# A two-layer decoder trunk on one core: the sixth weight remainder of an expert on POOL, the overflow placing in thirteen parts, and expert weights read in runs of 4 KB

## The reference, cut to what matters

```
x = x + hierarchical_moe(rms_norm(x, norm_ffn[l]), ...)

# D_MODEL = 1024, D_FF_EXPERT = 256, N_EXPERTS = 16, TOP_K = 2, DEPTH = 2, float32
for e in range(N_EXPERTS):
    hid = jax.nn.silu(t @ w_g[e]) * (t @ w_u[e])
    y = y + gates[:, e:e + 1] * (hid @ w_d[e])
```

## Time and profile before

| | before |
|---|---|
| median of 3 runs | 1600.07 us (1598.69 to 1601.12) |
| the profiled execution, its own time | 1602.11 us |
| its span | 1599.9 us |
| PE busy | 1460.6 us, 91% of the span |
| DVE busy | 931.6 us, 58% |
| ACT busy | 845.0 us, 53% |
| POOL busy | 446.9 us, 28% |
| chain that ended last | PE 67%, DVE 13%, issue 6%, ACT 5%, DMA 5%, POOL 3% |

### The profile page before, as it was taken

How to read it: one execution, slowest core, us unless ns; L and a number is a source line. 1 busy time by engine, 2 the same in 40 slices (tenths; PEclk the granted TensorE clock), 3 DMA queues, 4 the chain that set the end, 5 groups by cost and what they waited for, 6 DMA issues and landing times.

```text
span 1599.9 us, 22011 instructions
## 1 busy us (share of the span) xinstructions
PE 1460.6 (91%) x7636; PEld 1131.9 (71%) x7636; DVE 931.6 (58%) x1844; ACT 845.0 (53%) x1665; POOL 446.9 (28%) x634
## 2 busy tenths in 40 slices
PE   7999999999999995999689999999999999779993
PEld 5786777677767884777477867776677678667772
DVE  3544655534554446999654455645444535579995
ACT  4445555555443335888533555555554433558882
POOL 3314228320000025853005043284000000268210
PEclk9999999999999997999879999999999999989997
DMA  6822222112232366999566212221122332679995
GB/s 154 149 78 55 64 56 66 53 54 63 64 112 76 101 204 223 337 363 354 195 176 120 75 53 63 58 72 53 53 67 60 107 95 98 226 241 346 372 320 195
DMA packets 154325, 226.82 MB, mean 142 GB/s; under 512 B 20547, under 2 KB 89923, under 8 KB 154212
## 3 DMA queue, kind: packets, MB, share of 16 engines
q1 hardware_dynamic: 142724, 205.43, 42.2%
q0 software_dynamic: 10768, 17.80, 3.3%
q10 hardware_dynamic: 720, 2.16, 0.4%
HBM read 216.80 MB, written 25.49 MB: 151 GB/s over the span
## 4 chain that ended last, share of the span: by engine, by line
PE 67%; DVE 13%; issue 6%; ACT 5%; DMA 5%; POOL 3%; SPq 1%; ACTq 0%; POOLq 0%; DVEq 0%
PE bank L488 17%; PE bank L490 16%; PE bank L489 16%; PE bank L1399 4%; DVE xT L553 4%; PE bank L1384 3%; PE bank L1375 3%; PE bank L1377 2%; ACT xT L547 2%; DMA raw<-in_w_in_dram 2%; DVE oT L856 1%; POOL rsq L1970 1%; DMA rows<-ytok 1%; PE bank L1431 1%; PE bank L1434 1%
## 5 line engine op out<-in xcount | busy, mean ns | idle before, releaser
L488 PE MATMUL bank<-wh,xT 128*128 128x512 f32 (+1 forms) x960 | 401.5, 418 | 15.4 <-DVE xT L1743 5.3
L490 PE MATMUL bank<-wh,xT 128*128 128x512 f32 (+1 forms) x960 | 376.6, 392 | 0.0
L489 PE MATMUL bank<-wl,xT 128*128 128x512 f32 (+1 forms) x960 | 375.3, 391 | 0.0
L461 ACT ACTIVATE wh<-raw 128x512 fp32r<-128x512 f32 (+1 forms) x300 | 187.2, 624 | 330.1 <-PE bank L490 314.0
L467 DVE TENSOR_TENSOR wl<-raw,wh 128x512 fp32r<-128x512 f32 (+1 forms) x300 | 214.6, 716 | 245.8 <-ACT wh L461 235.1
L488 PEld LDWEIGHTS bank<-wh,xT 128*128 128x128 f32 x960 | 182.1, 190 | 83.3 <-issue 33.0
L490 PEld LDWEIGHTS bank<-wh,xT 128*128 128x128 f32 x960 | 181.7, 189 | 37.9
L489 PEld LDWEIGHTS bank<-wl,xT 128*128 128x128 f32 x960 | 182.9, 191 | 30.6 <-issue 1.4
L1542 ACT ACTIVATE prob<-prob,nmax 128x128 f32<-128x128 f32 (+3 forms) x192 | 107.2, 560 | 124.5 <-DVE nmax L1755 124.0
L1755 DVE CUSTOM_DVE_ANT_0 prob<-bank,mask 128x128 f32<-128x128 f32 (+3 forms) x128 | 60.6, 489 | 187.6 <-PE bank L1375 98.6
L2078 POOL TENSOR_TENSOR rows<-x_rows,ac 128x512 f32<-128x512 f32 x16 | 21.9, 1405 | 514.6 <-DVE x_rows L1826 514.6
(11 more groups left out here) (328 smaller groups left out, 2545.7 us busy)
## 6 DMA issues: line engine op xcount, KB each, us to landing
raw<-in_w_in_dram SPq DMA_DIRECT2D x192, 256.0 KB, 2.7
bqkv<-in_w_expert_gate_dram SPq DMA_DIRECT2D x64, 256.0 KB, 4.9
bqkv<-in_w_expert_up_dram SPq DMA_DIRECT2D x64, 256.0 KB, 6.0
bqkv<-in_w_expert_down_dram SPq DMA_DIRECT2D x32, 512.0 KB, 7.2
q_c<-in_w_expert_gate_dram SPq DMA_DIRECT2D x64, 256.0 KB, 5.4
q_c<-in_w_expert_up_dram SPq DMA_DIRECT2D x64, 256.0 KB, 6.8
head_odd<-in_w_expert_down_dram SPq DMA_DIRECT2D x32, 512.0 KB, 6.9
raw<-in_w_branch_dram SPq DMA_DIRECT2D x48, 256.0 KB, 2.6
```

Of the source, the lines that this page charges most:

```text
L461: nc.scalar.activation(wh[:, i % HL, 0:width], raw[:, i % RAW, 0:width], ACT.Copy).then_inc(hi_ready, 1)
L488: nc.tensor.matmul(out, lhs[0], rhs[0], start=start, stop=False)
L489: nc.tensor.matmul(out, lhs[0], rhs[1], start=False, stop=False)
L490: return nc.tensor.matmul(out, lhs[1], rhs[0], start=False, stop=stop)
```

## The change

Five things change together.

1. The remainder of pair 5 (the second half of down) of experts 0 to 14 is made by POOL and no longer by DVE, with a semaphore of its own (`last_lo_ready`).
2. POOL's order becomes: four gathers first; then in each step e the remainder of pair 5, the gather of expert e + 4, the scatter of expert e, one part of the placing, and in layer 0 two gains. The placing has thirteen parts (steps 0 to 12) where it had six, with the same operations; its product on PE moves from step 9 to step 13.
3. Gate and up are loaded with four transfers of 512 KB where there were eight of 256 KB, and a partition reads 4 KB in one run where it read runs of 1 KB. A partition then holds rows 8p to 8p + 7 of the weights, and so the token rows are written in that order by POOL (`by_eight`: the same operation with the output strided). Down is loaded in two transfers as before, in runs of 4 KB where there were runs of 2 KB.
4. A pair of down is now one half of the contraction (k) and all 1024 columns, where it was both halves and 512 columns. PE goes through k first: the first half for both halves of the columns, then the second half for both.
5. The semaphore counts follow.

```diff
         def pair_lo(e, j, par, half):
+            eng, done = (nc.gpsimd, last_lo_ready) if j == 5 else (nc.vector, pair_lo_ready)
             pair, landed, count = pair_place(e, j, par, half)
-            nc.vector.wait_ge(pair_hi_ready, of(pair_hi_ready, pair_no(e, j) + 1))
-            nc.vector.wait_ge(landed, of(landed, count))
-            nc.vector.tensor_tensor(pair_w[:, pair_ring(e, j, par), 1], pair,
-                                    pair_w[:, pair_ring(e, j, par), 0].bitcast(F32),
-                                    ALU.subtract).then_inc(pair_lo_ready, 1)
+            eng.wait_ge(pair_hi_ready, of(pair_hi_ready, pair_no(e, j) + 1))
+            eng.wait_ge(landed, of(landed, count))
+            eng.tensor_tensor(pair_w[:, pair_ring(e, j, par), 1], pair,
+                              pair_w[:, pair_ring(e, j, par), 0].bitcast(F32), ALU.subtract).then_inc(done, 1)
...
-        def load_gate_up(sp, expert, j, par, s_):
+        def load_gate_up(sp, expert, quad, par, s_):
+            ms = slice(1024 * quad, 1024 * (quad + 1))
             for half, w in ((0, "w_expert_gate"), (1, "w_expert_up")):
-                src = at(t[w].rearrange("l e (k p) f -> (l e) p k f", p=P), expert)
-                sp.dma_start(pair_raw[par][j][:, :, half * FF:(half + 1) * FF], src[:, 2 * j:2 * j + 2, :]).then_inc(s_, 16)
+                src = at(t[w].rearrange("l e (p k) f -> (l e) p (k f)", p=P), expert)
+                sp.dma_start(gate_up_raw[par][:, half, ms], src[:, ms]).then_inc(s_, 16)
...
         def experts_pe(pe):
...
-                for c in range(2):
-                    j = c if is_const(e, NE - 1) else 4 + c
-                    pos_wait(pe, y_read[c], of(y_read[c], e))
-                    pe.wait_ge(pair_lo_ready, of(pair_lo_ready, pair_no(e, j) + 1))
-                    down(y_bank[c][:], pair_ring(e, j, par)).then_inc(y_done, 1)
+                for k in range(2):
+                    j = k if is_const(e, NE - 1) else 4 + k
+                    pair_split(pe, e, j)
+                    for c in range(2):
+                        if k == 0:
+                            pos_wait(pe, y_read[c], of(y_read[c], e))
+                        mm = down(c, k, pair_ring(e, j, par))
+                        if k or c:
+                            mm.then_inc(y_done, 1)
...
         def experts_act(act):
...
-                act.wait_ge(y_done, of(y_done, 2 * e + 1))
+                act.wait_ge(y_done, of(y_done, 3 * e + 2))
                 pos_wait(act, y_out[par], of(y_out[par], 16 * half))
                 nc.scalar.activation(ysb[:, par, 0:512], y_bank[0][:], ACT.Copy).then_inc(y_read[0], 1)
...
         def experts_dve(dve, layer):
...
                     pair_lo(e, 4, par, half)
-                    pair_lo(e, 5, par, half)
                     silu(e + 1, 1 - par)
...
         def experts_pool(pool, layer):
...
-            for e in range(NE):
-                if e >= 2:
-                    pool.wait_ge(xg_turned, of(xg_turned, 2 * (e - 1)))
-                gather(xg[:, e % 2, :], tab_i[:, e:e + 1], xg_in[e % 2])
-                if e >= 4:
-                    home(e - 4)
-                if 2 <= e < 8:
-                    place_overflow(pool, e - 2)
-                if e >= 4 and layer + 1 < DEPTH:
-                    for q in range(2 * (e - 4), min(N_GAINS, 2 * (e - 3))):
+            for e in range(4):
+                rows_of(e)
+            for e in range(NE):
+                if e < NE - 1:
+                    pair_lo(e, 5, e % 2, e // 2)
+                if e + 4 < NE:
+                    rows_of(e + 4)
+                home(e)
+                place_overflow(pool, e)
+                if layer + 1 < DEPTH:
+                    for q in range(2 * e, min(N_GAINS, 2 * e + 2)):
                         load_gain(pool, layer + 1, q)
```

More of the change, by code:

```diff
@@ L317, in build @@
         RAW_SEMS = [sem(f"raw_in{i}") for i in range(RAW)]
-        pair_in = [[sem(f"pair_in{b}_{j}") for j in range(6)] for b in range(2)]
+        pair_in = [[sem(f"pair_in{b}_{j}") for j in range(4)] for b in range(2)]
         xg_in = [sem(f"xg_in{b}") for b in range(2)]
@@ L373, in build @@
             PER_LAYER[f"y_read{b}"] = NE
-            for j in range(6):
-                PER_LAYER[f"pair_in{b}_{j}"] = (32 if j < 4 else 16) * NE // 2
+            for j in range(4):
+                PER_LAYER[f"pair_in{b}_{j}"] = (32 if j < 2 else 16) * NE // 2
         for n in range(NT):
@@ L616, in body @@
                 expert = sp.value_load(ctl[0:1, bass.ds(c, 1)], min_val=0, max_val=NE - 1)
-                for j in range(4):
-                    load_gate_up(sp, layer * NE + expert, j, 0, ovs[now[0]]["w"])
+                for quad in range(2):
+                    load_gate_up(sp, layer * NE + expert, quad, 0, ovs[now[0]]["w"])
                 for q in range(2):
@@ L633, in body @@
                 pe.wait_ge(ovs[now[0]]["hT"], c + 1)
-                for q in range(2):
-                    pe.wait_ge(ovs[now[0]]["lo"], 6 * c + 5 + q)
-                    down(y_bank[q][:], (4 + q) % 3).then_inc(ovs[now[0]]["used"], 1)
+                for k in range(2):
+                    pe.wait_ge(ovs[now[0]]["lo"], 6 * c + 5 + k)
+                    for q in range(2):
+                        mm = down(q, k, (4 + k) % 3)
+                    mm.then_inc(ovs[now[0]]["used"], 1)
             overflow(pe, body)
@@ L1091, in place_overflow @@
                     step(tt(ovc, ovc, extra, ALU.add))
+            elif part == 1:
                 step(copy(incl, ovc))
@@ L1104, in place_overflow @@
                     step(tt(q_, q_, place, ALU.add))
+            elif part == 3:
                 step(tt(place, over, over_n(extra), ALU.mult))
@@ L1116, in place_overflow @@
                 step(ins)
+            elif part == 7:
                 ts(over_tok[:, :, 0, :], over_eq, tok_id[:, 0:1], None, ALU.mult)
                 tt(over_tok[:, :, 1, :], over_eq, tile_no.unsqueeze(2).broadcast_to([P, m8, n_ov]), ALU.mult)
[L1119 to L1121 removed]
+                step(tt(over_tok[:, :, 2, :], over_eq, home_no.unsqueeze(2).broadcast_to([P, m8, n_ov]), ALU.mult))
+            elif part in (8, 9, 10):
+                for m in range(3 * (part - 8), min(m8, 3 * (part - 7))):
                     ins = ts(over_row[:, m, :], rank_of, row[:, m:m + 1], None, ALU.is_equal)
[L1123 to L1126 removed]
+                if part == 10:
+                    ins.then_inc(r_ranked, 1)
+            elif part == 11:
                 for c in range(n_ov):
@@ L1129, in place_overflow @@
                 step(ins)
+            elif part == 12:
                 summed(few[0:1, 2, 0:n_ov].unsqueeze(2), cmp)
@@ L1220, in _ @@
                 for e in range(2):
-                    for j in range(4):
-                        load_gate_up(sp, layer * NE + e, j, e, pair_in[e][j])
-                    for c in range(2):
-                        load_down(sp, layer * NE + e, c, e, pair_in[e][4 + c])
+                    for quad in range(2):
+                        load_gate_up(sp, layer * NE + e, quad, e, pair_in[e][quad])
+                    for k in range(2):
+                        load_down(sp, layer * NE + e, k, e, pair_in[e][2 + k])
                 for n in range(NT):
```

97 lines of the change are left out of this document (48 added, 49 removed).

## The result

The changed kernel takes 1647.68 us (median of 4 runs, 1641.3 to 1654.26) against 1599.68 us before (1598.69 to 1601.12, 4 runs): a ratio of 1.03, with a 95% interval of 1.025 to 1.0349. The profiled execution of after took 1643.37 us, its span is 1641.5 us.

The account below looks back on a forecast made before the run. It took a chain over DVE, ACT and PE, 10.26 us a step, to bound the kernel. Layer 0's loop 22.5, layer 1's 9.3 and clock 5.5 gave 37 us on 1602.1: 1638 us, range 1604 to 1685.

Parts of the forecast that it names:

- The round through POOL: Closed loop of POOL's remainder, PE, ACT's copies, scatter, placing and gains: 12.1 us with placing and gains, 10.9 with placing alone.
- Remainder done to the first columns on ACT: Loop stretch from the end of POOL's remainder through three matmuls on PE to ACT's copy: 1.0 us.
- 11 long rounds: Layer 0's 11 steps with both placing and gains on POOL: 12.1 us each, 1.85 us added per step.
- The part of the placing: One part of the overflow placing on POOL in each loop: 16.3 us over five parts, 3.3 us, DVE's remainders included.
- The clock: PE drops to the lower clock after pauses in the long steps: 0.5 us in each of 11, 5.5 in all.
- A step without placing: An expert step with nothing else on POOL: 10.65 us, 0.4 over the kernel before.
- Late first columns: Down by contraction half delays ACT's first copy and the rounding of pair 1 behind it: PE stands 0.6 to 0.75 us.
- the gain of DVE: Moving pair 5's remainder off DVE lets its gate start earlier: 0.46 us a step.
- Costed at nothing: Longer load runs, POOL's strided rows, the placing's product in step 13 and fewer issues on SP: 0 us.
- Exclusion of DVE and POOL: DVE's remainders and POOL's operations hold each other off; 0.3 us a loop for DVE in the way of POOL's remainder.
- POOL keeps up and the late columns decide: Rival: placing parts stay short, so 30 steps cost 0.3 to 0.4 us each: 1609 to 1612 us, chance 0.15.
- The faster case: Rival: DVE's gain stands, 13 us, 1587; or longer runs relieve full DMA engines, 28 us; chance of both ways 0.12.

Follow-up runs that it names:

- dve5: The changed kernel with the remainder of pair 5 made by DVE again, all else kept: 1612.5 us, ratio 1.0060 to the kernel before.
- copylate: The changed kernel with ACT rounding pair 1 of the next expert before its first copy of the result, not between the two copies: 1624.6 us, ratio 1.0151.
- lag: The changed kernel with POOL scattering in step e the result of expert e - 1 instead of expert e: 1625.3 us, ratio 1.0157.
- noplace: The changed kernel without the work of placing the overflow on POOL (three fills and the counter copies stay): 1620.9 us, ratio 1.0110.
- dve5_cl: The changed kernel with pair 5's remainder on DVE again and pair 1 of the next expert rounded before ACT's first copy: 1597.2 us, ratio 0.9974.
- cl_lag: The changed kernel with pair 1 rounded before ACT's first copy and POOL scattering expert e - 1 in step e: 1610.4 us, ratio 1.0057.
- dve5_cols: The changed kernel with pair 5's remainder on DVE again and down by columns as before, in 2 KB runs: 1600.5 us, ratio 0.9990.

## Why the prediction was right, and where its terms were off

**The round through POOL** was the cause, as said: dve5 takes POOL's remainder off it, copylate takes a rounding off it, lag opens it, and they give 35, 23 and 22 us. The sum was 37 us, measured 41 between the profiled executions, and by layers 28.0 and 9.3, measured 28.9 and 15.5. That layer 0 fits so well is luck: the clock and DVE in the way of POOL's remainder were put too high (by 3.6 and 3.3 us), the placing and the last steps too low (by 5.7 and about 3), and these errors cancel.

**Its terms,** in the step shown above. Remainder done to the first columns on ACT: 1.0 predicted, 1.33 measured (659.34 to 660.67, in a stretch at the lower clock; 1.05 at the upper). Copies and rounding: 2.0, measured 2.04. To the end of the scatter: 1.85, measured 1.84. Gains: 1.2, measured 1.2. The remainder: 2.4, measured 2.38. The 11 long rounds of layer 0 take 12.49 us in the mean, with the clock; 12.1 + 0.5 was predicted.

**The part of the placing** is the term that was too small: 3.3 us predicted, and 4.58 in this step (664.57 to the gains at 669.15). From the end of the scatter to the next remainder, less the gains, it is 3.8 us in the mean of the 11 long rounds of layer 0, and 3.9 in the 13 rounds with placing of layer 1. In layer 1, where no gains blur it, a part of the sums takes 4.0 us and the round 11.32, where 10.9 was predicted (chain of after; a round from one part of the placing to the next):

```profile
1502.84 1.78 POOL gate_t L1089 x2
...
1506.85 2.40 POOL xT L562
...
1514.16 1.79 POOL gate_t L1089 x2
```

The prediction spread 16.3 us over five parts; on the round each part begins right behind the scatter, where DVE makes its remainders. In the step shown the same operation of line 1118 takes 0.38 us at 666.26, and 1.34 at 667.12 while DVE makes this one (DVE's timeline):

```profile
667.00 1.23 DVE L562 TENSOR_TENSOR xT<-head_odd,xT 128x1024 fp32r<-128x1024 f32 x1 [0.52 <-ACT xT L555]
```

How much of the 0.5 us that the mean part is too long comes from this was not measured.

The 13 rounds of layer 1 with placing take 10.60 to 13.15 us, 11.35 in the mean, which is 5.9 of the 6.2 us that the sum lacks there. But 2.2 of these stand in the longest round alone, and not in its placing. Its scatter starts 2.46 us after the copy, where the others start after 0.78, and takes 1.74 us:

```profile
1476.55 2.46 issue
...
1479.00 1.74 POOL ytok L718
```

The third scatter of layer 1 comes late in before too (POOL stands 3.88 us ahead of it), where nothing on a round waits for it. No view names what POOL waits for, and the cause stays open.

**The clock.** 0.5 us for each of 11 long rounds, 5.5 in all, was too much. The stretches at the lower clock came in six of them, and cost the round 1.9 us. A seventh, which the prediction didn't have, lies over the last twelve matmuls of down in layer 0: these take 4.26 us (808.60 to 812.86), and 3.03 in before (784.51 to 787.54).

**A step without placing** was to be 10.65 us, and is (773.5 - 656.1) / 11 = 10.67. The last two steps take 17.3 us in noplace and took 14.3 before; these 3 us a layer the prediction didn't have (scatters of noplace in the middle and at the end of layer 0, then those of before at the end):

```profile
L718 POOL DMA_INDIRECT ytok<-ac,prob x12: 993/1028/1035, 656.1 to 773.5; - x12
L718 POOL DMA_INDIRECT ytok<-ac,prob x3: 975/982/985, 784.2 to 801.5; - x3
L708 POOL DMA_INDIRECT ytok<-ac,prob x3: 973/973/973, 774.6 to 788.9; - x3
```

Of the 3 us, 1.6 are the clock: the last twelve matmuls of down take 4.63 us in noplace, most of them at 0.50, and 3.03 in before.

**Late first columns** with ACT's order, 0.6 to 0.75 us a step, set against 0.46 gained. With the remainder on DVE nothing is gained, PE starts at 712.21 as in before, and the same arithmetic leaves 713.7 - (712.21 + 1.37) = 0.1; measured (150.9 - 147.8) / 15 = 0.2. dve5_cl shows that the cause is the one named, the rounding of pair 1 behind the copy. That the gain of DVE is there when all else is out of the way is shown by the 9.87 us steps of cl_lag: 0.39 under 10.26, against 0.46.

**Costed at nothing,** and rightly: the longer runs, the thirteen parts, the fewer issues (dve5_cols), and POOL's strided rows, which take 1.31 us in the median where the earlier trace rows has 1.30. (By the numbers of the earlier trace rows the packets in 4 KB runs are 12% faster and not 14, which changes nothing.)

**Exclusion of DVE and POOL** held, in the direction said, but the 0.3 us for DVE in the way of POOL's remainder did not come. POOL's remainders take 2.34 to 2.49 us, but for the last of each layer with 2.7, and DVE's stretches (POOL's remainders of one raw place in the whole run, then DVE's timeline while POOL's runs from 656.96 to 659.34):

```profile
L562 POOL TENSOR_TENSOR xT<-bqkv,xT x16: 2363/2403/2730, 631.4 to 1606.5; 128x1024 fp32r<-128x1024 f32 x16
...
657.37 3.05 DVE L562 TENSOR_TENSOR xT<-bqkv,xT 128x1024 fp32r<-128x1024 f32 x1
```

**The rivals.** That POOL keeps up and the late columns decide is what noplace shows when the placing is gone, at 1621 and not at 1609 to 1612. The faster case didn't come; the longer runs gave nothing in any run. How the 27 us of the placing split into its bare time and what DVE adds wasn't tried.

## What to carry to other kernels

Before work moves to an engine that "has time", write down what stands on that engine between two of the moved pieces, and whether anything there waits for what the moved piece releases. If it does, all of it lies on a round, and its length counts in every step, however idle the engine is on average (POOL was 28% busy). Cut or shorten such a round where it is cheapest: one rounding moved ahead of a copy gave 23 us, a scatter one step later 22, and neither changed the amount of work. And when two numbers agree, look for a second cause in the trace: 12.9 us against 12.8 looked as if the clock cost nothing, and the matmuls on the round showed 1.9 us. And price the parts of a change together: the order of down cost 12 us or 26, depending on who makes the remainder.

## What the runs showed of the hardware

- A subtract of 128x1024 with both inputs in SBUF takes 2.39 us on POOL and 1.23 on DVE.
- Where two such operations met, the one that ran first kept its length: DVE's of 1.23 us took 3.05 beside POOL's of 2.38 us.
- Starting a gather is held off as well. The median was 1.09 us before and 1.05 in noplace; in after a gather often begins while DVE still makes the remainder that POOL's had stretched (the one at 659.52 while DVE's runs to 660.42), and takes 1.9. That the remainder is what holds it is read from the times alone. Gathers of after, then of noplace:

```profile
L712 POOL DMA_INDIRECT ac<-xn_dram,tab_i x32: 984/1861/2146, 609.1 to 1576.2; - x32
L712 POOL DMA_INDIRECT ac<-xn_dram,tab_i x32: 984/1049/1783, 616.9 to 1558.2; - x32
```

- A stretch of 3.4 us at a granted clock of 0.50 cost the round 0.06 to 0.64 us, as three matmuls stood on it and PE had waits behind them. Over twelve matmuls of down in a row, with nothing to hide behind, it cost 1.2 to 1.6 us (4.26 to 4.63 against 3.03).
